# Compressed-attention pages loaded as whole rows by GpSimd and turned by VectorE in 32x32 blocks, in a one-core decoder step

## What is computed

```
blocks = kv_all[:, idx] + transpose(pe, (1, 0, 2))[:, :, None, :]      # windows of 32 tokens, stride 16
flat = transpose(blocks, (0, 1, 3, 4, 2, 5)).reshape(b, n_cmp, 2, G, 32 * 64)
hid = gelu(einsum('bncgf,cfh->bncgh', flat, w1))                       # 2048 -> 128
comp = einsum('bncgh,chd->bncgd', hid, w2)                             # 128 -> 64: k_c and v_c
```

## Time and profile before

| | us |
|---|---|
| median of 3 runs | 1554.99 |
| lowest and highest | 1551.15 and 1556.51 |
| the profiled execution | 1553.46 |
| its span, first to last instruction | 1551.8 |

### The profile page before, as it was taken

One profiled execution on the slowest core, in us unless ns is written; L12 is line 12 of the kernel. 1 busy time (PEld: TensorE's weight loads), 2 busy tenths in 40 slices (PEclk: granted clock), 3 DMA queues, 4 the chain that ended last, 5 costly groups with the idle time before them and its releaser, 6 DMA issues.

```text
span 1551.8 us, 21395 instructions
## 1 busy us (share of the span) xinstructions
PE 1436.0 (93%) x7528; PEld 648.2 (42%) x7528; DVE 473.3 (31%) x1079; ACT 293.3 (19%) x609; POOL 101.8 (7%) x217
## 2 busy tenths in 40 slices
PE   7998988888878899999999999999999999999986
PEld 3446554665756445433333333333333333333332
DVE  1114463334243365313213213213213213213214
ACT  2013333333333412111011101011011011010112
POOL 1002001432410000000000000000000000000000
PEclk9998989998989999999999999999999999999999
DMA  7328724775758765999999999999999999999993
GB/s 253 109 57 221 262 90 167 202 240 156 222 170 245 231 259 233 413 428 429 428 429 428 429 429 428 429 428 429 428 428 429 428 429 428 429 428 428 428 427 130
DMA packets 99291, 507.56 MB, mean 327 GB/s; under 512 B 30979, under 2 KB 45795, under 8 KB 74115
## 3 DMA queue, kind: packets, MB, share of 16 engines
q1 hardware_dynamic: 91170, 483.28, 77.9%
q0 software_dynamic: 8064, 23.60, 4.8%
HBM read 500.35 MB, written 10.62 MB: 329 GB/s over the span
## 4 chain that ended last, share of the span: by engine, by line
PE 69%; DMA 19%; DVE 5%; ACT 3%; issue 3%; SPq 1%; DVEq 0%; ACTq 0%
PE PS L1336 21%; DMA arena<-in_w_gate_up 18%; PE PS L1363 9%; PE PS L1310 5%; PE PS L343 5%; PE PS L599 4%; PE PS L2004 3%; PE PS L529 3%; PE PS L1302 3%; PE PS L1198 2%; PE PS L1054 2%; PE PS L352 1%; PE PS L572 1%; ACT arena L762 1%; PE PS L1947 1%
## 5 line engine op out<-in xcount | busy, mean ns | idle before, releaser
L1336 PE MATMUL PS<-arena 128*64 128x512 f32 x2048 | 457.6, 595 | 24.2 <-DMA arena<-in_w_gate_up 23.4
L1336 PEld LDWEIGHTS PS<-arena 128*64 128x64 f32 x2048 | 141.0, 137 | 309.0 <-issue 259.7
L1363 PE MATMUL PS<-arena 128*64 128x512 f32 x1024 | 226.0, 594 | 3.2 <-DVE arena L1819 2.3
L1778 DVE TENSOR_SCALAR arena<-PS 128x512 f32<-128x512 f32 x32 | 22.1, 692 | 489.4 <-PE PS L1345 488.4
L1363 PEld LDWEIGHTS PS<-arena 128*64 128x64 f32 x1024 | 72.1, 137 | 150.2 <-issue 147.6
L529 PE MATMUL PS<-arena 128*128 128x128 f32 (+1 forms) x624 | 98.5, 298 | 38.9 <-ACT arena L762 13.9
L529 PEld LDWEIGHTS PS<-arena 128*128 128x128 f32 (+1 forms) x624 | 73.2, 150 | 61.9 <-ACT arena L762 20.1
L1302 PE MATMUL PS<-arena 128*128 128x512 f32 (+1 forms) x192 | 79.4, 617 | 6.0 <-ACT arena L1506 6.0
L1310 PE MATMUL PS<-arena 128*128 128x512 f32 (+1 forms) x180 | 84.2, 608 | 0.0
L343 PE MATMUL PS<-arena 128*128 128x512 f32 (+1 forms) x192 | 78.7, 571 | 0.6 <-ACT arena L2185 0.6
L1491 ACT ACTIVATE arena<-arena 128x512 f32<-128x512 f32 x32 | 20.1, 630 | 293.0 <-DVE arena L1778 293.0
(11 more groups left out here) (287 smaller groups left out, 1295.6 us busy)
## 6 DMA issues: line engine op xcount, KB each, us to landing
arena<-in_w_gate_up SPq DMA_DIRECT2D x128, 2048.0 KB, 22.2
arena<-in_w_down SPq DMA_DIRECT2D x64, 2048.0 KB, 21.8
arena<-in_w_in SPq DMA_DIRECT2D x9, 2048.0 KB, 10.6
arena<-in_cache_diff_k SPq DMA_DIRECT2D x64, 256.0 KB, 4.7
arena<-in_cache_diff_v POOLq DMA_DIRECT2D x64, 256.0 KB, 4.2
arena<-in_cache_sel_kv SPq DMA_DIRECT2D x64, 128.0 KB, 2.1
arena<-in_cache_cmp_kv POOLq DMA_DIRECT2D x64, 64.0 KB, 4.6
arena<-in_cache_cmp_kv SPq DMA_DIRECT2D x64, 64.0 KB, 2.8
```

What stands on the lines that cost most here:

```text
L1336: last = nc.tensor.matmul(bank(2 + role + 2 * u)[64 * h:64 * h + 64], hTm[:, k, BS * u:BS * u + BS], gu_w[:, k, D * role + 512 * h:D * rol ...
L1363: last = nc.tensor.matmul(bank(6 + u)[64 * h:64 * h + 64], aT[u][:, c % 4, 64 * (c // 4):64 * (c // 4) + 64], down_w[u][c // 4][:, c % 4, ...
```

## The change

- **Pages.** A compressed page is loaded whole, one row of 256 floats to a partition, the tokens sorted by their remainder by 4 (partition 32 r + k holds token 4 k + r). GpSimd issues all of them. The buffer cmp_raw now holds the eight pages of one sequence; each load waits until VectorE has turned the page that was there.
- **Turning.** VectorE transposes each page in 32x32 blocks straight into cmpT (SBUF to SBUF), eight blocks of 32 columns to a page. The 32 page transposes of TensorE and their 8 evacuations a turn are gone, and with them "phase". A hidden product now contracts over four tokens of 32 features; w1 is loaded again in that order for the sample sequences (16 DMAs on SP, behind the prompt's hidden products).
- **Where it is turned.** The first sequence of pair 0 during prompt attention, the second ahead of the loop; in turn i those of pair i+1: the first sequence in two halves (behind the hidden products of the keys, and behind the copies of k_c and v_c), the second behind `dif_mask(1)`.
- **Order in a turn.** `sel_t` goes between the hidden products, the products for k_c and v_c ahead of `dif_values(0)`, window keys behind the compressed scores, `join(0)` behind them, the sum over heads ahead of the window scores; VectorE's choice of blocks goes ahead of its wait for the window scores. The hidden products of keys and values have a bank and a semaphore count each, and each ScalarE table load its own cell.
- **Start.** norm_mix is loaded as 8 rows and turned by TensorE with the first tile; tiles go 2 (sample), 0, 1; the squares of tiles 0 and 1 go behind the scaled copies.
- The group numbers, counts and semaphores follow.

```diff
-        cmpT = at(18432, 4, 2, CS // 2, PAST // CS)
+        cmpT = at(14336, 16, 4, PAST // CS)
-        cmp_raw = at(14336, NPAGE, 512)
+        cmp_raw = alloc(NPAGE, 256)
...
-        def cmp_rows(eng, pg, b, k, h, q):
+        def cmp_pages(eng, i, b, first=False):
             cmp_d = io["cache_cmp_kv"][0].rearrange("n p c g d -> n p (c g d)")
...
+            for pg in range(NPAGE):
+                page = page_of(eng, i, b, pg)
+                if b or not first:
+                    eng.wait_ge(cmp_turned, i * 16 + (8 * b - 7 + pg) if not first else pg + 1)
+                eng.dma_start(cmp_raw[:, pg],
+                              cmp_d[bass.ds(page, 1)].rearrange("a (k r) n -> (a r) k n", r=4)).then_inc(cmp_in[pg // 4], 16)
...
             with sp.Fori(1, PAIRS_OF_SEQ) as i:
-                cmp_pages(i)
                 dk_pages(i, 0)
...
             arrived(pool, "small")
-            pool.wait_ge(pj_full, 15)
-            odd_rows(0, True)
             out_done(pool, G_QK + 14)
             queries_of(0, True)
             for n in range(12):
...
+                if n == 5:
+                    pool.wait_ge(ph_full, 2)
+                    cmp_pages(pool, 0, 0, True)
+                if n == 11:
+                    cmp_pages(pool, 0, 1, True)
                 pool.wait_ge(gate_out, n + 1)
...
             with pool.Fori(1, PAIRS_OF_SEQ) as i:
-                odd_rows(i)
+                cmp_pages(pool, i, 0)
                 values_in(i, 0)
+                cmp_pages(pool, i, 1)
                 queries_of(i)
                 values_in(i, 1)
...
+            def turn_pages(i, b, cs=(0, 1)):
+                for pg in range(NPAGE):
+                    if pg % 4 == 0:
+                        dve.wait_ge(cmp_in[pg // 4], i * 128 + 64 * b + 64)
+                    m0, m1 = 4 * cs[0], 4 * cs[-1] + 4
+                    out = cmpT[:, 8 * b + m0:8 * b + m1, :, 8 * pg:8 * pg + 8].rearrange("p m r n -> p m n r")
+                    st(V.transpose(out, cmp_raw[:, pg, 32 * m0:32 * m1].rearrange("p (m d) -> p m d", d=32)), cmp_turned if 1 in cs else None)
...
-                ev(1, 3, 5, 7)
+                ev(1, 3)
+                if not final:
+                    dve.wait_ge(l_hid, i * 2 + 1)
+                    turn_pages(i + 1, 0, (0,))
                 past(dve, l_exp, i * 5 + 1)
...
+                ev(5)
                 dve.wait_ge(l_kv, i + 1)
...
+                if not final:
+                    turn_pages(i + 1, 0, (1,))
+                dif_scale(0)
...
                 dif_mask(1)
+                if not final:
+                    turn_pages(i + 1, 1)
 
                 past(dve, l_exp, i * 5 + 4)
...
                 dif_scores(0)
+                pe.wait_ge(cmp_turned, i * 16 + 16)
+                hidden(0, range(8))
+                sel_t(0)
+                hidden(0, range(8, 16))
+                sel_t(1)
+                hidden(1, range(16))
                 dif_probs_t(0)
...
+            sp.wait_ge(ph_full, 2)
+            for c in range(2):
+                for r, e in ((r, e) for r in range(4) for e in range(2)):
+                    load(sp, "w1_quads", w1[32 * r:32 * r + 32, c].rearrange("p (s e) h -> p s e h", e=2)[:, :, e],
+                         io["w_cmp1"][0, c].rearrange("(s r e p) h -> r e p s h", r=4, e=2, p=32)[r, e])
```

More of the change, by code:

```diff
@@ L422, in sync_attention @@
             kd_d = io["cache_diff_k"][0].rearrange("n p h c d -> n p (h c d)")
[L423 to L430, removed]
             def sel_pages(i, first=False):
@@ L690, in pe_attention @@
                 key_t(0, G_FIRST[pg], pg, 64)
+            arrived(pe, "w1_quads")
             l_out_done(pe, 0, -1)
@@ L811, in turn @@
                 if not final:
-                    table(ACT.Exp)
-                    ev(40)
+                    table(ACT.Exp, 3)
+                    ev(32)
             for n in G_FIRST[0::2]:
@@ L1948, in tp @@
                 last.then_inc(tp_full, 1)
-            arrived(pe, "first")
-            for t in range(3):
+            for k, t in enumerate(TILE_ORDER):
                 r = ROWS[t]
@@ L1954, in _ @@
                 for half in range(2):
-                    tp(2 * t + half, [(xin[0:r, t, 128 * (4 * half + k):128 * (4 * half + k) + 128], r * k) for k in range(4)])
+                    tp(2 * k + half, [(gmix_rows, 4 * r)] * (k + half == 0)
+                       + [(xin[0:r, t, 128 * (4 * half + m):128 * (4 * half + m) + 128], r * m) for m in range(4)])
             out_done(pe, G_PE - 1)
@@ L2176, in root, with square_of @@
                 st(nc.scalar.activation(v, v, ACT.Sqrt), root_ready)
-            arrived(act, "first")
-            for t in range(3):
+            def square_of(t):
+                st(nc.scalar.activation(at(31232 + 1024 * t, 1024)[0:ROWS[t]], xin[0:ROWS[t], t, :], ACT.Square, accum_out=ssq[0:ROWS[t], t:t + 1]),
+                   squares)
+            for k, t in enumerate(TILE_ORDER):
                 r = ROWS[t]
-                arrived(act, f"x{t}")
-                st(nc.scalar.activation(at(31232 + 1024 * t, 1024)[0:r], xin[0:r, t, :], ACT.Square, accum_out=ssq[0:r, t:t + 1]), squares)
-                act.wait_ge(tp_full, 2 * t + 1)
-                for k in range(4):
-                    st(nc.scalar.activation(xnT[:, k, 128 * t:128 * t + r], bank(0)[:, r * k:r * k + r], ACT.Copy,
-                                            scale=gmix[:, k:k + 1]), tp_out[0] if k == 3 else None)
-            for t in range(3):
+                act.wait_ge(tp_full, 2 * k + 1)
+                if k == 0:
+                    st(copy(gmix, bank(0)[:, 4 * r:4 * r + KD]))
+                    st.own()
+                for m in range(4):
+                    st(nc.scalar.activation(xnT[:, m, 128 * t:128 * t + r], bank(0)[:, r * m:r * m + r], ACT.Copy,
+                                            scale=gmix[:, m:m + 1]), tp_out[0] if m == 3 else None)
+                if k == 0:
+                    square_of(t)
+            for t in TILE_ORDER[1:]:
+                square_of(t)
+            for t in TILE_ORDER:
                 root(x_rstd[0:ROWS[t], t:t + 1])
```

194 lines of the change are left out of this document (91 added, 103 removed).

## The result

The changed kernel takes 1566.09 us (median of 4 runs, 1562.91 to 1567.37), the kernel before, on the same chip, 1555.51 us (4 runs, 1551.15 to 1556.51). The ratio is 1.007, with a 95% interval of 1.0046 to 1.0095. It is slower, where I had forecast 1545 us and faster, and it lies above my range. The profiled execution took 1562.91 us, with a span of 1561.3 us (before: 1551.8) and a mean granted clock of 0.967 (0.980).

What follows compares the result with a forecast made beforehand. The full-bandwidth expert stage only slides; TensorE's chain and an issue-queue wait bound the loop. Turn 0 +12.7, turns 1 and 2 -10.4, turn 3 -8.2, start -2.3 sum to -8.2 us: 1545 us, range 1527 to 1563.

Steps and rivals of the forecast that it cites:

- the landing: Time from a page's last issue in the loop until it has arrived: 3.3 us taken, ends 2.2 and 5.3.
- (a): Second sequence's pages, issued behind diff values on GpSimd: 26.1 us (10.5+8.8+3.3+1.5+2.0) where TensorE needs 19; 7 us idle.
- turning and combination: VectorE's work after the last landing: four page transposes, 1.5 us, then the NSA combination, 2.0 us.
- The rule of the Trainium skill: DMA engines per page: largest number up to 16 dividing both outermost sizes; four landings would cost 0.9 us more each, 1549.
- (b): Lower clock after the new idle costs 2.2 us: NSA rows to end of second values take 6.3+2.2 = 8.5 us.
- (c): First sequence's pages, from second values to the next first values: 26.6 us against TensorE's 28.5, hidden by 1.9.
- Turn 0: First loop turn pays 12.7 us: late pages move first values from 292.2 to 301.0, the boundary from 328.0 to 340.7.
- Turn 3: Last loop turn fetches no pages, so it takes 8.2 us less.
- The small edits: Page turning in the loop (some 7 us) hidden, w1 reload in time, table buffers and gelu split cost nothing.
- The start: norm_mix loaded as rows: the projection starts at 12.5, not 14.85, for 2.3 us less; ends 0 and 2.8.
- Rival 2: No change: pages land late, at 5.3 us, whatever their cut; +8 us, 1553; chance 0.15.
- a slower rival only for the issue interval: GpSimd issues pages 1.71 us apart, not 1.26: +18 us, 1563; slower from 1.62; chance 0.18.

Runs made afterwards that it cites:

- e1_rows16: The changed kernel with each page's rows taken in token order (outermost size 128, not 4): 1548.13 us, ratio 0.9947.
- e8_r16: The changed kernel with each page's rows cut 16 ways, not 4: 1555.85 us, ratio 0.9994.
- e7_table_only: The changed kernel with ScalarE's load of the exponential's table after the second gelu put behind the next two evictions: 1564.72 us, ratio 1.0068.
- e3_start_only: The kernel before with the start edits alone (norm_mix as rows, sample tile first, squares behind the first copies): 1555.07 us, ratio 0.999.
- e10_turn_late: The changed kernel with VectorE's turning of the second sequence's pages moved behind the finished rows: 1548.3 us, ratio 0.9963.
- e5_pages_first: The changed kernel with GpSimd issuing second-sequence pages before first-sequence values, and the next pair's first-sequence pages before second-sequence values: 1535.96 us, ratio 0.9868.
- e11_order_table_late: e5_pages_first plus the table load behind the next two evictions and second-sequence page turning behind the finished rows: 1517.8 us, ratio 0.9767.

## Why the prediction was wrong

By the loop's end I had forecast 8.2 us less; it is 10.9 us more. The 19.1 us between them are X, the stretch from the first values to the finished rows, 11.8; turn 3, 3.9; the way to turn 1's first values, 2.0; turn 0 up to its first values, 1.1; the rest, 0.3. Of the 11.8, 10.8 are the landing. Point by point:

- **(a), the size that failed: the landing.** In turn 1 the last page is issued 19.3 us behind the first values (369.4 to 388.69), my 10.5+8.8 (10.2+9.2 by its parts). Then the landing took 6.6 where I took 3.3, and turning and combination 3.7 where I had 3.5. X was 30.45, 29.7 and 29.95 us, not 26.1: 11.8 us over three turns. I had chosen 3.3, "nearer the low one since the pages are no longer cut into 256-byte runs". Longer runs didn't help against a cut in four, and 7.2 lies above my upper end of 5.3: both rows that I bounded it by were half pages with 64 outermost rows. e1_rows16 measures the step: 2.8 to 3.0 us with 128 rows outermost, which would have made my 3.3 good. There TensorE idles 7.7 us before the finished rows for my 7, turns 1 to 3 take 63.8, 64.1 and 50.3 us for my 63, 63 and 46, and the time is 7.6 us under the kernel before, for my 8.2. So the path was right and this term was wrong.
- **The rule of the Trainium skill** pointed the right way, and my estimate for it was 0.9 us a landing, from bandwidth. The Trainium skill, DMA: Bandwidth & Descriptors, "Why a DMA increments its semaphore by 16 and not by 1", lets the size of the slowest dimension set the number of engines. e8_r16 agrees in direction: 16 pieces in place of 4 take 2.5 us off the landing, nearly three times my price. The remaining 1.4 us that e1_rows16 takes off lie outside that rule. That pages were served by four engines each was not seen directly.
- **(b) held**: Z, from the finished rows to the end of the second values, was 8.65, 8.4 and 9.0 us for my 8.5, with the low clock that I charged for: 0.61 in the wait in turn 0 and 0.56 from 331.0 to 338.9 us behind it.
- **(c) held in turns 2 and 3** (28.6 and 28.3 us for 28.5), but it took 30.5 before turn 1's first values. In the quiet stretches the landing of 3.3 was right (medians 3.3 and 3.6). The 2.0 us too many are not the queue: TensorE waits 0.24 us there, with the pages turned just in time. It is the granted clock, 0.93 in this stretch and 1.00 in turns 2 and 3, which fell on the first values themselves (64 products in 3.46 us against 1.96 in turn 2).
- **Turn 0**: the first values ended at 299.8 us. I had 301.0, or 298.7 with the 2.3 us of the start taken off. The mixture was another, and that the sum came near is partly luck. I forecast one idle stretch of 9 us before the first values; there were 2.7 us, and 4.2 before the hidden products, which I had at nothing, with a low clock (0.54) on the 16 products behind it. GpSimd's last page was issued at 289.80 for my 292.7. Where the wait before the hidden products was 1.1 us, in e1_rows16, the one before the first values was 7.1.
- **Turn 3**: 4.3 us less, not 8.2. I had taken the gain from turn 0's stretches. Up to the first values it took 23.5 us for my 23.4, and X was 19.6 for my 19.3, but the kernel before needed only 25.5 and 23.6 in its own turn 3, not 26.6 and 24.4, which is 1.9 of the missing 3.9 us. 0.4 are the two excesses, and 1.6 are the last 72 value products at a lower clock (3.51 against 1.95 us for the first 64).
- **The small edits** cost what I said as the kernel stands, as e7_table_only shows, but not for my reason. The load of the exponential's table stalls TensorE by 1.69 us in every turn; ScalarE doesn't hide it, the late pages do. With them gone it costs 5 us. GpSimd's issues (1.31 us apart for my 1.26), the turning (1.9 us for the four pages behind the last landing, for my 1.5) and SP's new loads, all in time, were sized nearly right.
- **The start** gave 0.9 us at the projection for my 2.3: the wait that I had left open, the first part of w_in, is there (2.13 us idle, released by in_w_in). e3_start_only bounds the whole part at 3 us (0.2%).
- **The rivals.** Rival 2, late landings, is nearest to what came, and my sign for it, landings over 4 us, showed. But it had them late "whatever their cut", and e1_rows16 shows that the cut decides. Its price was too small: 5.3 us in four landings and "no change", when three took 6.6 to 7.2. These alone bring the forecast from -8.2 to +2.6 us, which is still its "no change"; the other terms of the 19.1 us above made it slower. I had a slower rival only for the issue interval, at 1.62 us and more; it was 1.31.

What I missed above the sizes is that (a) itself was a choice of the change. I took the two lists as given and summed along them. X is 19 us of TensorE's work and some 11 us of waiting for pages that nobody needs before the next turn. The landing was the term that decided the sign, but the two orders were the larger loss: e10_turn_late gains 18 us with the slow landing left in, e5_pages_first 30, and e11_order_table_late 48 with the cut in four and all of the change's operations.

## What to carry to other kernels

In an engine's in-order list, a wait for data of the next iteration belongs behind every instruction that feeds the bottleneck in this one; sum the lists as they stand, then ask what each wait stands in front of. When a transfer changes the size of its outermost dimension, take the landing of rows with that size, or keep a wide upper bound: bytes and run length didn't give it. Ask too what else is loading then: the cut in four landed in 3.3 to 3.6 us in quiet stretches and in 7.0 in busy ones. And try a small stall again after the large one is gone: the same edit of the table load was worth nothing before and 5 us after.

## What the runs showed of the hardware

- The last 128 KB page of a second sequence, issued by GpSimd beside other loads, landed in 6.6 to 7.2 us with an outermost size of 4, in 3.5 to 5.2 with 16 over rows 16 KB apart, and in 2.8 to 3.0 with 128 rows in order. The last page of turn 0's first sequence, with little else under way, took 3.8, 2.4 and 2.3 us. The cut in four also had 96 packets more a page, each under 512 bytes. Why, stays open.
- GpSimd's issue of such a page was 0.68 us long for the cut in four, 0.52 for 16 and 0.55 for 128 rows; the distance between issues stayed 1.31 us in all.
- VectorE turns a 128x256 fp32 page in 32x32 blocks in about 0.48 us (3.79 us for eight), a 128x256 fp32 product took 0.42.
- Idle time of TensorE went with a lower granted clock. With equal operations, the loop's busy time was 199.8 us at 0.79 to 0.97 and 66.9 us of idle time, and 186.1 us at 0.97 to 1.00 and 25.5 us of idle time.
